# Cached keys turned in 32 by 32 blocks on VectorE and scored with a spread query; second norm reordered

## The reference

```python
def moba_attend(q, kb, vb, t, slopes):          # per sequence: 8 heads, 4 queries, blocks of 256 tokens
    qf = q * (B_HEAD_DIM ** -0.5)
    kbar = jnp.mean(kb.astype(jnp.float32), axis=2)
    g = jnp.einsum('hqd,hnd->hqn', qf.astype(jnp.float32), kbar)      # gate of each past block
    ...                                                               # top 3 of 4 past blocks, and the own one
    s = jnp.einsum('hqd,hqnkd->hqnk', qf, ks).astype(jnp.float32) - slopes[:, None, None, None] * dist
    s = jnp.where(valid[..., None] & (dist >= 0), s, NEG)
    p = jax.nn.softmax(s.reshape(H, q.shape[1], -1), axis=-1).reshape(s.shape)
    return jnp.einsum('hqnk,hqnkd->hqd', p.astype(vs.dtype), vs)
```

## Time and profile before

| | |
|---|---|
| median of 3 runs | 1229.33 us (1228.59 to 1230.97) |
| the profiled execution, its own time | 1227.56 us |
| its span | 1225.8 us |
| PE busy | 1177.5 us, 96% |
| DVE busy | 715.4 us, 58% |
| ACT busy | 563.7 us, 46% |
| loaded and stored | 324.87 MB, mean 265 GB/s |

### The profile page before, as it was taken

The page is one execution under the profiler, slowest core; times in us unless marked ns, Lnnn a source line. Parts: engine busy times, 40 slices in busy tenths (PEclk is TensorE's granted clock), DMA queues, the critical chain, the costliest instruction groups (busy, mean ns, idle before and its releaser), DMA issues.

```text
span 1225.8 us, 23735 instructions
## 1 busy us (share of the span) xinstructions
PE 1177.5 (96%) x9352; PEld 1041.6 (85%) x9352; DVE 715.4 (58%) x1356; ACT 563.7 (46%) x713; POOL 332.2 (27%) x207
## 2 busy tenths in 40 slices
PE   5899999999999999999999998899999989999997
PEld 2689798878888787788788898799999989999997
DVE  3746555545544546534445456489999996583112
ACT  3333323333344444422343236566666656575443
POOL 1000000000000002200000004467766678705773
PEclk9999999999999999999999999999999999999998
DMA  9999899999898878899999998385848445454542
GB/s 334 338 338 337 281 334 309 376 364 344 287 315 301 284 257 296 271 374 315 335 373 340 323 329 231 114 292 154 289 149 285 137 138 179 143 176 157 164 146 94
DMA packets 236962, 324.87 MB, mean 265 GB/s; under 512 B 12429, under 2 KB 152525, under 8 KB 236429
## 3 DMA queue, kind: packets, MB, share of 16 engines
q1 hardware_dynamic: 233472, 312.78, 76.0%
q0 software_dynamic: 2192, 7.79, 2.2%
q10 hardware_dynamic: 1188, 2.79, 0.7%
HBM read 317.96 MB, written 7.06 MB: 265 GB/s over the span
## 4 chain that ended last, share of the span: by engine, by line
PE 75%; DVE 16%; DMA 4%; issue 2%; ACT 2%; SPq 1%; POOL 0%; DVEq 0%; ACTq 0%
PE PS L307 18%; PE PS L311 18%; PE PS L310 18%; DVE PS L1751 10%; PE PS L395 6%; PE PS L987 4%; PE PS L1014 3%; DMA XR<-in_ada_w 3%; PE PS L1245 2%; DVE WLO L301 1%; DMA WRAW<-in_c_w_in 1%; PE PS L505 1%; PE PS L410 1%; ACT WHI L296 1%; DVE HL L1671 1%
## 5 line engine op out<-in xcount | busy, mean ns | idle before, releaser
L307 PE MATMUL PS<-HH,WHI 128*128 128x288 f32 x2176 | 662.0, 304 | 15.3 <-DVE HL L454 4.1
L311 PE MATMUL PS<-HH,WLO 128*128 128x288 f32 x2176 | 643.2, 296 | 0.0
L310 PE MATMUL PS<-HL,WHI 128*128 128x288 f32 x2176 | 642.9, 295 | 0.0
L296 ACT ACTIVATE WHI<-WRAW 128x1024 fp32r<-128x1024 f32 x272 | 283.7, 1055 | 348.5 <-PE PS L311 295.8
L307 PEld LDWEIGHTS PS<-HH,WHI 128*128 128x128 f32 x2176 | 410.1, 188 | 37.8 <-issue 31.7
L310 PEld LDWEIGHTS PS<-HL,WHI 128*128 128x128 f32 x2176 | 410.7, 189 | 0.0
L311 PEld LDWEIGHTS PS<-HH,WLO 128*128 128x128 f32 x2176 | 409.8, 188 | 0.0
L301 POOL TENSOR_TENSOR WLO<-WRAW,WHI 128x1024 fp32r<-128x1024 f32 x117 | 281.1, 2424 | 195.6 <-ACT WHI L296 195.6
L301 DVE TENSOR_TENSOR WLO<-WRAW,WHI 128x1024 fp32r<-128x1024 f32 x155 | 190.0, 1227 | 159.6 <-ACT WHI L296 159.3
L1751 DVE SCALAR_TENSOR_TENSOR PS<-ACTS,CWT,PS 128x288 f32<-128x288 f32 x448 | 192.4, 516 | 0.0
L1727 ACT ACTIVATE ACTS<-ACTS 128x1088 f32<-128x1088 f32 x32 | 70.3, 2197 | 60.7 <-DVE ACTS L1749 34.8
(11 more groups left out here) (280 smaller groups left out, 753.9 us busy)
## 6 DMA issues: line engine op xcount, KB each, us to landing
XR<-in_ada_w SPq DMA_DIRECT2D x192, 512.0 KB, 8.6
WRAW<-in_ab_w_in SPq DMA_DIRECT2D x112, 512.0 KB, 7.9
WRAW<-in_c_w_in SPq DMA_DIRECT2D x96, 512.0 KB, 3.6
XR<-in_cache_b_k SPq DMA_DIRECT2D x128, 256.0 KB, 5.3
XR<-in_cache_b_v SPq DMA_DIRECT2D x128, 256.0 KB, 5.8
WRAW<-in_ab_w_out SPq DMA_DIRECT2D x32, 512.0 KB, 8.6
WRAW<-in_c_w_out SPq DMA_DIRECT2D x32, 512.0 KB, 3.4
ACTS<-in_x_prompt ACTq DMA_DIRECT2D x2, 1024.0 KB, 10.8
```

Of the source, the lines that this page charges most:

```text
L296: act.activation(WHI[:, i % 4], WRAW[:, i % 4], ACT.Copy).then_inc(w_hi, 1)
L307: first = pe.matmul(out, whi, HH[:, k, :], start=start, stop=False)
L310: pe.matmul(out, whi, HL[:, k, :], start=False, stop=False)
L311: return pe.matmul(out, wlo, HH[:, k, :], start=False, stop=stop)
```

## The change

**Keys.** DVE turns the keys instead of PE. Its transpose (`k_turn`, new L1009) turns every 32 by 32 block in place of the whole tile, 128 partitions x 512 elements at a time, from `XR` straight to `KT`. After it partition 32i + d of `KT` holds channel 32e + d of the tokens of quarter i, at columns chosen by e. The query is therefore spread: `BD` holds for each sequence, head and channel quarter e a weight of 32 columns which is block diagonal over the token quarters i (`q_spread` on PE copies the query to all four partition quarters through pieces of the identity, `q_fill` on DVE and ACT puts it into the zeroed `BD`). A head is now 16 matmuls of 64 columns, summed over e (`k_scores`). The 128 rows of the scores are sequence x head parity x token quarter x query, with four head pairs in the free dimension, and a row holds a quarter of the tokens of four heads. The two banks M0 and M2 take turns by unit. ACT and DVE copy no keys any more.

**Softmax.** A row is a quarter, so sums and maxima are joined over four rows: gates and Z by a matmul with a 0/1 matrix `SAME` (`gate_sum`, `z_sum`), maxima by a transpose to four partitions, a reduce, and a transpose back (`max_turn`, `max_fold`, `max_back`, `max_take`). exp is four instructions a half, 1/Z is applied to the probabilities by four ACT instructions (`row_norm`), and `probs_turn` is 132 matmuls of 32 columns in place of 9 transposes. For the second half these steps stand at m = 0 to 9 of the v stage, and the steps of branch A behind them up to four m later.

**Order in the k stage.** A unit has 16 pieces of dense product on PE; a head's scores stand behind every second. An `XR` buffer is freed by DVE after the fourth head of its half, so two buffers together. The LayerNorm of branch A is earlier (units 3, 5 and 6).

**Second norm.** On ACT `pair_square(5)` stands before `hi(145)`, the last pair is squared by ACT and not by DVE, `hi(146)` and `hi(147)` stand behind the fourth and the eighth of the new inputs `HH`; five of the eight state copies stand before them. On PE the state is turned mostly behind the sum.

The core of the diff:

```diff
-        def k_turn(pe, u, c, g4):
-            g, hh, j2 = 16 * u + 4 * c + g4, 2 * (c // 2) + g4 // 2, g4 % 2
-            if g >= 2:
-                pe.wait_ge((kt_a, kt_d)[g % 2], g // 2)
-            for h2 in range(2):
-                for t in range(2):
-                    at = 512 * (2 * j2 + t) + P * ((2 * hh + h2) % 4)
-                    last = pe.transpose(PS[:, (M2, M3)[g % 2], (2 * h2 + t) * P:(2 * h2 + t + 1) * P],
-                                        XR[:, c, at:at + P], IDENT[:])
-            last.then_inc(kt_tr, 1)
+        def k_turn(dve, u, h):
+            half, x = h // 4, h % 4
+            if 8 * u + h >= 2:
+                dve.wait_ge(ks_head, 8 * u + h - 1)
+            for c in (2 * half, 2 * half + 1):
+                if x == 0:
+                    dve.wait_ge(x_rdy[c], need(17 + u, c))
+                last = dve.transpose(KT[:, h % 2, 4 * (c % 2):4 * (c % 2) + 4, :],
+                                     XR[:, c].rearrange("p (a n) -> p a n", a=4)[:, :, P * x:P * x + P])
+                last.then_inc(kt_tr, 1)
+                if x == 3:
+                    dve.wait_ge(kt_tr, 16 * u + 2 * h + c % 2 + 1)
+                    dve.sem_inc(x_used[c], 1)
...
+        def q_spread(pe, b):
...
+            for e in range(4):
+                for i in range(4):
+                    for s in range(4):
+                        last = pe.matmul(PS[32 * i:32 * i + 32, M3, P * e + 32 * s:P * e + 32 * s + 32],
+                                         IDENT[:, 32 * e:32 * e + 32], rhs[:, s], start=True, stop=True)
...
+        def k_scores(pe, u, h):
+            g, h2, bank = h // 2, h % 2, (M0, M2)[u % 2]
+            pe.wait_ge(kt_tr, 16 * u + 2 * h + 2)
+            if h == 0:
+                if u > 1:
+                    pe.wait_ge(ks_free, u - 1)
+                if u % 4 == 0:
+                    pe.wait_ge(s_bdf, 8 + 2 * u)
+            for e in range(4):
+                for j in range(4):
+                    x = (4 * e + j) * 4 + g
+                    last = pe.matmul(PS[32 * j:32 * j + 32, bank, 64 * g:64 * g + 64], BD[:, x, 16 * h2:16 * h2 + 32],
+                                     KT[:, h % 2, 2 * j:2 * j + 2, 32 * e:32 * e + 32],
+                                     start=h2 == 0 and e == 0, stop=h2 == 1 and e == 3)
+            last.then_inc(ks_head, 1)
...
         def row_exp(act, b):
             act.wait_ge(s_max, b + 1)
-            act.activation(SROW, SROW, ACT.Exp, bias=NMAX, accum_out=ZSUM).then_inc(s_exp, 1)
+            for g in range(4):
+                act.activation(SROW[b][:, g, :], SROW[b][:, g, :], ACT.Exp, bias=NMAX[:, g:g + 1],
+                               accum_out=ZSUM[:, g:g + 1]).then_inc(s_exp, 1)
...
             for q in range(16):
+                if q == 15:
+                    pair_square(act, 5)
+                    pair_scaled(act, 4)
                 hi(act, 115 + 2 * q)
...
-                hi(act, 116 + 2 * q)
-                if q >= 10:
+                if q < 15:
+                    hi(act, 116 + 2 * q)
+                if 10 <= q < 15:
                     pair_square(act, q - 10)
...
         def norm1_act(act):
             pair_square(act, 6)
+            pair_scaled(act, 5)
             act.activation(RT[:, 2:3], RT[:, 3:4], ACT.Sqrt)
-            hi(act, 4 * P_AB + 3)
             pair_scaled(act, 6)
-            for f in range(3):
-                state_copy(act, f)
+            act.wait_ge(s_res, 16)
+            act.wait_ge(n1_add, 5)
+            act.activation(SQ2[7 % 3], XT[:, 14:16, :], ACT.Square).then_inc(n1_last, 1)
             pair_scaled(act, 7)
```

More of the change, by code:

```diff
@@ L1066, in k_pe @@
                         last.then_inc(s_sqmm, 1)
-            k_scores(pe, 7, 3)
         def silu_zt(act, job, x):
@@ new lines, in k_act, with key_bias @@
+                if u == 6:
+                    row_norm(act, 0)
+                hi(act, 68 + 2 * u)
+                if u == 5:
+                    row_exp(act, 0)
+                    root(act, 2)
+                if u == 6:
+                    for f in range(3):
+                        probs_save(act, 0, f)
+        def key_bias(dve):
+            dve.wait_ge(s_iota, 1)
+            for g in range(4):
+                dve.tensor_scalar(ALB[:, g, :], IOTA, TOKROW, SLOPE[:, g:g + 1], ALU.add, ALU.mult)
```

495 lines of the change are left out of this document (291 added, 204 removed).

## The result

| | before | after |
|---|---|---|
| median | 1230.14 us (1228.59 to 1230.97, 4 runs) | 1259.99 us (1252.73 to 1265.87, 4 runs) |
| ratio | | 1.0226, 95% interval 1.0178 to 1.0274 |
| profiled execution, its own time | 1227.56 us | 1265.87 us |
| its span | 1225.8 us | 1264.1 us |

What follows compares the result with a forecast made beforehand. PE was taken as the bound, busy 96% of the span. k stage -15, v stage +5, second norm -5 against 1227.56 gave 1212.5, so 1214 us against a median of 1229.33; 8 in 10 range 1196 to 1238.

Steps and rivals of the forecast that it cites:

- Bound of the k stage before: k stage before: PE sets it, busy 147.7 of 152 us, with 15% of DMA to spare.
- the dearer price of 0.8 us a head: k stage scores: some 60 cycles of overhead on each pass would make a head 0.8 us and PE 127 us.
- The rival of slow transposes: k stage, DVE: at 1.13 us a transpose the stage grows 46 us, total 1275; decides from 0.77 us; chance 0.09.
- I add 7 us over the stage for the units in which DVE is light and the keys come last: k stage: 6.2 us of transfer against 7.5 us of DVE work per buffer pair is tight, so +7 us.
- Transfers take the gain: k stage: buffer pairs land 1.5 us late, stage 147, total 1221 to 1227; chance 0.15, plus 0.05 within 0.2%.
- Its sign, over 10 us of waiting for keys: k stage: DVE idle for `in_cache_b_k` by more than 10 us would point to transfers taking the gain.
- 1 to 2 us each, 8 in all: k stage: DVE loses its lead waiting for PE five times, with transposes behind each wait, +8 us.
- the five waits that were counted: k stage, DVE for PE: mean at (3,0), second filling of `BD`, `max_fold`, `max_take`, `z_invert`; 8 us in all.
- The other two terms of the v stage: v stage: +2 us for buffers left emptier by the k stage, +1.2 us for four single matmuls with breaks.
- PE's clock falls: k stage: 1.2 GHz for half the stage, PE needs 169 us, +17, total 1246; gaps of 1 to 2 us against it; chance 0.06.
- Second norm: Second norm: reciprocal 4 us after the last output product, first product about 6.5 us sooner, gain 5 us (3 to 7).
- +1 to +2 us: After the second norm: POOL's `lo(146)` and `lo(147)`, 2.4 us each, beside DVE's `HL` may hold it, +1 to +2 us.

Runs made afterwards that it cites:

- the neighbour on the same chip: Keys and softmax of the change put into the kernel before, second norm as before: 1268.57 us, ratio 1.0261, k stage 174.6 us.
- e4: Changed kernel with the small matmuls of `q_spread` and `probs_turn` cut into runs of 16 between dense pieces: 1260.87 us, ratio 1.0191.

## Why the prediction was wrong, point by point

- **Bound of the k stage before, and the rates of the new operations: right.** Transposes were forecast at 0.60 us a step and take 0.58 to 0.64 back to back; DVE was to be busy 120 to 131 us and is 127.7; a head's scores were forecast at 0.58 and take that (the dearer price of 0.8 us a head did not come). The rival of slow transposes fell. That PE would do its part in 113 us was low: it is busy 121.5 us even with DVE and transfers light.
- **"I add 7 us over the stage for the units in which DVE is light and the keys come last": the step that failed.** DVE waits 21.5 us for keys, not 7. The step compared 6.2 us of transfer with 7.5 us of DVE's work, and put SP's own work at nothing. What stands between DVE's low part and new keys is a chain through SP's queue, 14.8 us in the round shown: a weight load that waits for that low part, 4.3 us of page numbers, 4.3 of issues, 5.4 of transfer. Moving the numbers shortened the stage by 6 us (11 against the neighbour on the same chip) and halved DVE's wait for keys; taking the bytes out of the changed kernel gave 20 us. The rival "Transfers take the gain" had the transfers but not SP's queue, and sized them at 10 (stage 147): it is 169. Its sign, over 10 us of waiting for keys, came true.
- **"1 to 2 us each, 8 in all" for DVE's waits for PE: too small, and at other places.** DVE's idle time behind PE is 15.7 us. Of the five waits that were counted, only the second filling of `BD` (1.7) and `max_fold` (1.8) show. The two long ones stand at transposes, 3.9 us until 359.0 and 5.4 until 498.5, each a few us behind one of PE's stops for instructions. So the k stage is DVE's 127.7 us of work, 21.5 for keys and 15.7 for PE, and some 4 of small gaps, against 120 + 7 + 8 + 2.
- **`q_spread` and `probs_turn`: a run of 32 does not price a run of 128.** 21.6 ns a matmul (two passes) came from a run of 32. `probs_turn` keeps that price up to the first stop; `q_spread`, for which the forecast allowed up to four times as much, takes 42 ns. With the stops, for which there was no term, a pass takes 28 ns over the 256 of `probs_turn` and 49 over the 128 of the first `q_spread`, and the lower clock stands behind. This is 9.3 us in the v stage, which the forecast had at 2.0, and 8.3 us of stops in these two in the k stage. The other two terms of the v stage (2 us for emptier buffers, 1.2 for single matmuls) came to 1.1 together.
- **"PE's clock falls": it did, to 0.87, and it does not explain the stage.** The rival's stage of 169 us is the measured one by luck: it had PE busy for all of it, and PE is busy 127.9 us and waits 41. Its "gaps of 1 to 2 us" are up to 6.9 here. Fillers brought the clock back and lengthened the stage; what the lower clock costs by itself was not separated from them.
- **Second norm: right at its place, half at the end.** By itself: reciprocal at 3.9 us (forecast 4), first product 6.4 sooner (6.5), 3.0 left (5). The "+1 to +2 us" for low parts beside DVE was the mis-sized term: 2.8 of the 3.4 given back (two groups of 5.4 us in place of 4.0). In the 13 profiles with this edit 468.1 to 471.6 us follow the last output product, 469.0 in the median, against 471.2 before. The changed kernel's own profile has 471.2, so nothing is left there: the state that PE turns ahead of the last sum came late (a wait of 1.4 us for its transfer), and at 824.8 ACT waited 2.9 us for weights.

## What to carry over

When a buffer's user moves to another engine, follow the ring all the way: who frees it, what stands ahead of the load in the issuing queue, what each issue and register load costs there, and the transfer; compare that sum, not the transfer alone, with the work between two uses. Price a hundred short matmuls by a run of a hundred, and lay them between long ones if there is no such row. Limits that lie 5 to 10% under a stage's length are not slack: the waits between them add up. Ask what the stage is with each taken out.

## What the hardware showed that was not expected

- In long runs of short matmuls PE runs out of instructions. After 113 to 186 passes of a run, and then every 128, it stops for 1.7 to 5.5 us in the kernels that are not split (0.7 to 4.6 with few key bytes), until 1.2 to 1.6 us behind the landing of a 16 KB packet of instructions; 28 ns a pass over 256, 36 over 512, where 10 to 11 ns are seen between the stops (21 in `q_spread`). The second `q_spread` got through 128 passes without one. Sixteen matmuls (32 passes) between dense pieces cost 0.57 us a group (e4: 0.98 from one group to the next, a piece included, 0.40 for a piece), with one stop of 1.3 us left in eight groups.
- SP needs 0.55 us to read one page number into a register; an issue of a transfer takes it 0.33 us, and the next one starts 0.5 us after it (one took 1.04).
- Beside a low part on GpSimd some DVE operations with two inputs take far longer (L1696 1.7 in place of 0.29 us; the addition of 576 columns 2.87 in place of 0.76), while the transposes, with one input, do not change (690 ns for 512 columns).
- The start of an execution takes 41 us in the profile of before and 50.5 in that of the norm alone, with the same code: twelve transposes of the rows take 2.24 us in one and 3.51 in the other, eight matmuls of `ada_sum` 1.06 and 1.94. What decides is open: an expectation above calls it the lower clock, but the granted clock in the windows reads 1.00 in both.
